# One half tile of the next projection placed ahead of each head's chain, and the pooled products half a unit later

## The reference, cut to what matters

```python
z = h @ w_in
u_pool, q, k, v, o, i_pre, f_pre, ga, gb = jnp.split(z, idx, axis=-1)
y_a = pool_mixer(u_pool, w_pool, pool_scale) @ w_br_a   # per group of 4:
#   (window mean of u - u) @ w_pool[g], windows 2, 4, 8, 16, times pool_scale
q = silu(causal_conv(q, conv_q)); k = silu(causal_conv(k, conv_k))
hm = mlstm_chunkwise(q, k, v, i_pre, f_pre)             # 4 heads of 128
hm = sigmoid(o) * head_layernorm(hm, g_head)
y_b = hm @ w_br_b
merged = sigmoid(ga) * y_a + sigmoid(gb) * y_b
return merged @ w_out
```

## Time and profile before

| | |
|---|---|
| median of 3 runs | 3573.23 us |
| the three runs | 3568.24, 3573.23, 3577.52 us |
| span of the profiled execution | 3572.6 us |
| TensorE busy | 3425.6 us (96%) |
| VectorE busy | 1974.0 us (55%) |
| ScalarE busy | 1559.2 us (44%) |
| GpSimd busy | 180.4 us (5%) |

### The profile page before, as it was taken

The page is one execution under the profiler, slowest core; times in us unless marked ns, Lnnn a source line. Parts: engine busy times, 40 slices in busy tenths (PEclk is TensorE's granted clock), DMA queues, the critical chain, the costliest instruction groups (busy, mean ns, idle before and its releaser), DMA issues. The chain is left out here.

```text
span 3572.6 us, 54793 instructions
## 1 busy us (share of the span) xinstructions
PE 3425.6 (96%) x23462; PEld 2748.2 (77%) x23462; DVE 1974.0 (55%) x2532; ACT 1559.2 (44%) x1820; POOL 180.4 (5%) x179
## 2 busy tenths in 40 slices
PE   7999999989999999799999999999999999999998
PEld 5787676776666666587888888888788887888886
DVE  4544444455555555457556775355656657663444
ACT  4322110345555554344355664444433457654533
POOL 0000000000000000100010000000000011000000
PEclk9899999999999999899999999999999999999999
DMA  5100343358999998412110111053222111011333
GB/s 206 48 27 36 120 157 122 122 202 320 373 368 372 366 371 328 178 48 89 60 61 31 60 72 54 26 205 130 77 71 83 49 61 49 28 75 48 142 123 106
DMA packets 95913, 488.14 MB, mean 137 GB/s; under 512 B 10752, under 2 KB 11264, under 8 KB 57776
## 3 DMA queue, kind: packets, MB, share of 16 engines
q1 hardware_dynamic: 77216, 417.31, 31.6%
q0 software_dynamic: 12688, 46.27, 3.6%
q10 hardware_dynamic: 5760, 20.97, 1.4%
HBM read 427.23 MB, written 57.28 MB: 136 GB/s over the span
## 5 line engine op out<-in xcount | busy, mean ns | idle before, releaser
L136 PE MATMUL ps<-HH,WS 128*128 128x512 f32 (+1 forms) x2608 | 1046.4, 401 | 11.9 <-DVE WS L1387 9.4
L138 PE MATMUL ps<-HH,WS 128*128 128x512 f32 (+1 forms) x2608 | 1022.5, 392 | 0.0
L137 PE MATMUL ps<-HL,WS 128*128 128x512 f32 (+1 forms) x1968 | 772.1, 392 | 0.0
L136 PEld LDWEIGHTS ps<-HH,WS 128*128 128x128 f32 (+1 forms) x2608 | 493.2, 189 | 126.2 <-DVE WS L1387 12.5
L138 PEld LDWEIGHTS ps<-HH,WS 128*128 128x128 f32 (+1 forms) x2608 | 492.2, 189 | 107.6
L1450 ACT ACTIVATE WA<-ps 128x512 f32<-128x512 f32 x240 | 142.4, 594 | 801.5 <-PE ps L138 708.0
L137 PEld LDWEIGHTS ps<-HL,WS 128*128 128x128 f32 (+1 forms) x1968 | 372.5, 189 | 75.2 <-issue 1.0
L1387 DVE TENSOR_TENSOR WS<-RAW,WS 128x1024 fp32r<-128x1024 f32 (+1 forms) x153 | 200.7, 1313 | 161.1 <-ACT WS L1382 161.1
L136 PE MATMUL ps<-WS,HH 128*128 128x256 f32 x896 | 262.8, 293 | 13.4 <-DVE HL L2315 12.2
L137 PE MATMUL ps<-WS,HH 128*128 128x256 f32 x896 | 255.7, 285 | 0.0
L138 PE MATMUL ps<-WS,HL 128*128 128x256 f32 x896 | 255.6, 285 | 0.0
(11 more groups left out here) (413 smaller groups left out, 5197.5 us busy)
## 6 DMA issues: line engine op xcount, KB each, us to landing
WR<-in_weu SPq DMA_DIRECT2D x37, 1024.0 KB
WR<-in_weg SPq DMA_DIRECT2D x35, 1024.0 KB
WR<-in_wed SPq DMA_DIRECT2D x34, 1024.0 KB
RAW<-in_wo SPq DMA_DIRECT2D x32, 1024.0 KB, 4.9
H<-in_wed SPq DMA_DIRECT2D x26, 1024.0 KB, 9.0
WA<-in_wada SPq DMA_DIRECT2D x48, 512.0 KB
H<-in_weg SPq DMA_DIRECT2D x23, 1024.0 KB, 7.8
H<-in_weu SPq DMA_DIRECT2D x21, 1024.0 KB, 7.1
```

The lines of the kernel that those rows point to most:

```text
L136: t.matmul(o, l[0], r[0], start=st, stop=False)
L137: t.matmul(o, l[0], r[1], start=False, stop=False)
L138: return t.matmul(o, l[1], r[0], start=False, stop=sp)
```

## The change

`weave` takes one step of `prep` before the chain's first step and counts it. For h = 0 to 3 that moves exactly one half tile (or one step of values, or the first half of u0) from behind the chain's first step to ahead of it, on all engines and in the plan; the order of all later steps is the same. After head 3: one half, chain 1, two halves, chain 2, two, chain 3, three, chain 4, two, chain 5, two.

In the pooled part the product of group gi - 1 moves on TensorE from behind the first half of u(gi) to behind the second, and that of group 3 from behind the second half of ga0 to behind the first half of gb0. On VectorE the scaling of group 3 comes behind the split of the next weight instead of ahead of it; the others stay in their steps. The plan follows.

```diff
 def weave(core, prep, n_core, n_prep):
-    done_c = done_p = 0
-    alive = prep is not None
+    done_c = 0
+    alive = next(prep, 0) is None
+    done_p = 1
     for _ in core:
         done_c += 1
         while alive and done_p * n_core < done_c * n_prep:
@@ plan_pool
                 next(steps)
+                yield
+                next(steps)
                 if gi:
                     pooled(gi - 1)
-                yield
-                next(steps)
                 for n in range(1 + (gi > 0)):
                     wa.take("win", gi, n)
                 yield
@@ plan_pool, gates
             next(gates)
             yield
             next(gates)
+            yield
+            next(gates)
             pooled(3)
```

## The result

The changed kernel takes 3552.22 us (median of 4 runs, 3550.32 to 3559.17), the one before 3572.11 (4 runs): a ratio of 0.9943 with a 95% interval of 0.9929 to 0.9957, or 19.9 us less. The forecast was 3554.

A forecast was written before the change was run, and what follows sets the result against it. TensorE was taken to bound the kernel, with its idle and low-clock time to be won: 6.3 + 5.5 + 7.1 = 18.9 us off the 3572.6 us span, forecast median 3554 us, range 3547 to 3567.

The forecast's parts named there:

- The six waits: TensorE's three score waits for the SiLU (6.3 us) and three pooled-product waits for the windowed sums (5.5 us) all go.
- The order of ScalarE and VectorE behind the moved half: In the head chains, weight split and eviction now precede the exponentials; mask done at 10.8 us, in time; cost 0.
- margin of 6.6 us: Time from the mask's end (10.8 us) to the k tile's first half reusing a scores bank (17.4 us).
- The pooled products: Moved half a unit later, they find the windowed sums done; all 5.5 us of waits go, group 2's margin 3.5 us.
- The clock: Behind the waits of heads 1 to 3 and pooled group 2, 8.8 us lost; 7.1 us come back after one new fall.
- the sum: Whole count of gains in the head chains and pooled mixer: 6.3 + 5.5 + 7.1 = 18.9 us.
- The rule of the skill: Only idle gaps longer than these lower TensorE's clock; by it small matmuls caused the falls, which would remain.
- The gain reaches the end: After 387 us TensorE has no gap until routing and paces what follows, so the gain carries through.
- C: Rival: gain given back in the expert stage, waiting for weights; gain 0 to 8 us, time 3565 to 3573; chance 0.11.
- The border of measurement: Measurement of the whole kernel tells about 0.3% (10.7 us) from no change; faster means below 3562.5 us.

The follow-up runs named there:

- e1: Kernel before with only the weave's first step taken ahead of the chain, pooled products left in their old place; 3560.98 us, ratio 0.9966.
- e2: Kernel before with only the pooled products half a unit later, the weave left old; 3564.15 us, ratio 0.9971.
- e12: Changed kernel with 45 tiny ScalarE instructions ahead of each head's exponentials, 10.5 us in all; 3562.62 us, ratio 0.9975 to the kernel before.
- e11: Changed kernel with 15 tiny ScalarE instructions ahead of each head's exponentials, 3.5 us in all; 3555.82 us in one run.
- e4: Changed kernel with the engines keeping the old order at head 0; 3552.68 us, ratio 0.9944 to the kernel before.
- e6: Kernel before with its six gaps on TensorE filled by products of 4 rows that count for nothing; 3571.26 us in one run.
- e5: Kernel before with its six gaps on TensorE filled by dense matmuls that count for nothing; 3567.00 us, ratio 0.9979.
- e7: Changed kernel with two steps of the next projection ahead of the chain's first step instead of one; 3548.51 us, ratio 0.9928 to the kernel before.

## Why the prediction was right

- **The six waits.** Right: 6.3 and 5.5 us, each group removed by its own edit (e1, e2).
- **The order of ScalarE and VectorE behind the moved half.** At head 2 the exponentials ended 9.6 us after the projection (9.4 predicted), the mask at 10.4 (10.8), the k tile started at 17.6 (17.4). The margin of 6.6 us was put too small, since the bank awaited is that of the mask's first half, done at 9.4: 8.2 us, and e12 (exponentials some 10 us late, wait 1.9) agrees. One thing was missed: at head 3 VectorE takes group 0's windowed sum ahead of the mask, and the bank is needed by the second pair of row products already. There the mask's first half ends at some 296.9 us and the second product starts at about 298.1, a margin near 1 us. It didn't matter here, and e11's 3.5 us on ScalarE didn't reach it, because the mask there waits for VectorE's own queue: the exponentials are done at 285.7, the mask starts at 296.3. It is the thinnest place of the new order.
- **The pooled products.** Group 2's sum was done 9.1 us after u2's end (318.94 to 328.06; 9.2 predicted), and 3.5 us before its product, at 331.59, as predicted. Group 3's was done 4.9 us ahead (4.1).
- **The clock.** The mis-sized term. 7.1 us were to come back; in the first profile 10.5 did. For heads 1 to 3 and the pooled part the size held: 8.8 us back, one new fall of 1.7 us. Its place didn't: the sum priced it at the moved row products and scores, and it came behind head 1's transposes and second row products, which the sum didn't count. That one fall makes up the price is in part luck; of the eight profiles with one half tile ahead and no added wait, seven have one fall at head 1 (five at this place, two at the scores) and e4 has none. The difference is head 0, whose 5.2 and 1.7 us were taken to stay and of which 3.4 remained. But that is not shown to be a gain of the change: with the old order head 0 lost 1.7 us in e2, e4 and e6 and 6.8 in the first profile and in e5, 3.7 in the mean; with the new order 3.4 in each of six profiles (the changed kernel's three, e1, e11, e12). One execution of the kernel before had stood for all. So a part of the stage's 23.1 us is the luck of one profile, and the times' 19.9 us are nearer to the sum's 18.9.
- **The rule of the skill.** The Trainium skill (TensorE: Matmul & The Clock Gate, section Why this matters for your kernels) warns of longer idle gaps alone. By the runs, what stood in gaps of about 2 us mattered too: filling them with dense matmuls brought the clock back at two of three heads (e5), and with small ones at none (e6).
- **The gain reaches the end.** Right; against C stand the 3187.1 and 3188.6 us behind the stage and, over all profiles, 3183.5 to 3193.2 us behind a stage that ended 9 us or more earlier than before the change, against 3187.1 to 3199.3 behind the others. TensorE's one wait for a DMA before 1500 us is 6.5 us, where it was 6.8.
- **The border of measurement.** Over the 14 profiles, what follows the stage took 3183.5 to 3199.3 us with the same instructions. This, not the stage, which agreed within 0.1 us in three profiles of the changed kernel, is what makes 4 us impossible to tell.

## What to carry to other kernels

Where one engine is the bound and each wait in its order has a known length, a unit of independent work moved ahead of the wait wins the wait, and the length of the cover can be read off the other engine's timeline beforehand. Count also what the idle time does to the clock of the matmuls behind it: here it was nearly as much again. And follow the move through the buffers' order on each engine, head by head: the thinnest margin was at the one head whose companion work differs.

## What the runs showed of the hardware

Products with 4 rows of contraction kept TensorE "busy" in the profile but did not hold the granted clock at 2.4 GHz, as idle time had not (e6: 0.72 to 0.79 at heads 1 to 3). Scores and transposes of full height between two pairs of them held it at one head of three (e7). With the same instructions in the same order the falls came at the same places in three executions of the changed kernel (within 0.4 us, counted from the stage's start), while changes elsewhere moved them: in e11, where TensorE's own order is the same and only ScalarE has more to do, the fall at head 1 came 10 us earlier.
